# Four rows of a decode page to a partition, position sums over quads, and other buffers for the last value groups

## The chip, the cores and the metric

The kernel runs on one core of one Trainium2 chip. The metric is the device time of one execution in microseconds (us). Before the change it is 3598.28 us, the median of three runs (3588.35 to 3599.67).

## What is computed

One inference step of a two-layer decoder trunk. In each layer a prompt of 1024 tokens and a sample of 8 sequences with 8 new tokens each go through an input projection, three mixers side by side (retention, stick-breaking attention, forgetting attention), an output projection and a gated per-layer embedding. For the sample, both attentions also read a paged past: 32 pages of 128 rows for each of the 8 sequences, 5 heads of 64 numbers to a row, all in float32. The two formulas that matter here are:

```
z    = q @ k.T / 8                               # k: all 4096 past rows, then the new ones
stick-breaking: A[t,s] = exp(log_sigmoid(z[t,s]) + sum over s < j < t of log_sigmoid(-z[t,j]))
forgetting:     A[t,s] = softmax_s(z[t,s] + C[t] - C[s]),  C = cumulative sum of the log forget values
o    = A @ v
k    = cache_k[layer, page_table[sequence]]      # 32 pages of (128, 5, 64), the same for v
```

Stick-breaking so needs, for each past row, the sum of softplus(z) over all later rows, and forgetting attention the sum of the log forget values over all later rows.

## The kernel before

The program is written by engine: SP and POOL mostly issue DMAs, PE (TensorE) does matmuls and transposes, ACT and DVE move results out of PSUM and do elementwise work. Semaphores order them. A layer has eight phases; two of them are the decode stages, one for each kind of attention ("sb" for stick-breaking, "fox" for forgetting). With two layers there are four decode stages in a run.

**Loads.** A page is 128 rows of 320 numbers. Keys are loaded by SP (`load_k`, line 553), a few of the first sequence by ACT (line 1536), values by POOL (`load_group`, line 730). Eight pages make a group, four groups a sequence. Page p of a group lands in columns p*320 to p*320+319 of a buffer, one row to a partition on all 128 partitions. There are two key buffers (`ringK`, one in the weights' tile W, one in the tile named branch) and two value buffers (`ringV`). A key group's load waits until the blocks of the group two before it have been turned (`kt_ready`, line 551), a value group's until the group two before it has been weighed (`v_used`, line 728). The last sequence's value groups 2 and 3 are loaded by SP into the key buffers, which are free by then (lines 572 to 577).

**Keys to scores.** PE turns each group in five blocks of 128 key numbers by four pages (`turn_blocks`, line 1117), taken from PSUM by ACT (line 1548) or DVE (line 2069). It multiplies them with the queries (`score`, line 1139); ACT copies the result out (line 1556), PE turns it again so that the rows of a page lie on partitions (`turn_rows`, line 1153), and DVE puts it into `zs`, 128 partitions by 40 query rows by 33 slots, a slot being a page and the last one the new rows (`drain`, lines 2081 to 2088).

**Scores to weights.** For stick-breaking, DVE and ACT make softplus(z) (`soft`), and DVE's scan over the slots from the last to the first makes `later`, the sum over this and all later slots on the same partition (line 2107). `fold` (lines 1169 and 1170) adds for each row what lies on other partitions: six matmuls of 440 columns, three with the triangular constant `earlier` on `soft` and three with minus one on `later`. DVE adds the result to `zs` (line 2119) and ACT takes the exponential (line 1571). For forgetting attention, `page_sums` and `forget_sums` make the sums within and over the pages once a stage, PE turns them in ten transposes (`turn_forget`, line 1100) and DVE copies them out (line 2012); per sequence there is one small matmul in `fold` (line 1176). `weigh` (line 1202) multiplies the weights with a value group: 40 small matmuls to a group on four strips of PE.

**Order of the work.** All engines run `sequence(b, b - 1, b - 2)` in a loop. PE turns and scores the keys of sequence b, and in between folds and weighs groups 0 to 2 of sequence b-1 and group 3 of sequence b-2. PE's order in a pass is written out by hand (lines 1223 to 1258). The first sequence has nothing before it. After the loop PE weighs group 3 of sequence 6, folds sequence 7 and weighs its four groups (lines 1264 to 1268).

Of the kernel before, what the change touches and what calls it, by code (L numbers as in the profile page):

```python
# [24 lines left out]
ALU = mybir.AluOpType  # L25
# [22 lines left out]
GROUPS = PAGES // PG8  # L48
HI = HA * NEW
# [84 lines left out]
def tables():  # L134
# [17 lines left out]
    t["later_page"] = (j // PAGES == i // PAGES) & (j > i)  # L152
# [47 lines left out]
DECODE_STEPS = {"sb": 3, "fox": 5}  # L200
# [33 lines left out]
def step_program(nc, x_prompt, x_sample, state_ret, cache_sb_k, cache_sb_v, cache_fox_k,  # L234
# [10 lines left out]
    with ExitStack() as ctx:  # L245
# [210 lines left out]
        forget_turned = sem("forget_turned")  # L456
        forget_ready = sem("forget_ready")
# [64 lines left out]
        def _(sp):  # L522
# [3 lines left out]
            sp.dma_start(page_rows[:], page_table.rearrange("(a b) p -> (b p) a", a=2),  # L526
                         allow_slow_non_contiguous=True).then_inc(rows_in, 16)
# [18 lines left out]
            def load_k(L, kind, b, g, pages_of_group=PG8):  # L546
# [5 lines left out]
                for p, pg in enumerate(page_numbers(mybir.EngineType.SP, b * PAGES + g * PG8, pages_of_group)):  # L552
                    sp.dma_start(ringK[g % 2][:, p * DA:(p + 1) * DA],  # L553
                                 cache[L, bass.ds(pg, 1)].rearrange("a s h d -> s (a h d)"))\
                        .then_inc(s[f"k{g % 2}"], 16)

            def decode_loads(L, kind):
# [13 lines left out]

                for g in range(2, GROUPS):
                    sp.wait_ge(s["kt_ready"], (SEQS - 1) * BLOCKS + 5 * (g + 1))
                    for p, pg in enumerate(page_numbers(mybir.EngineType.SP, (SEQS - 1) * PAGES + g * PG8, PG8)):
                        sp.dma_start(ringK[g % 2][:, p * DA:(p + 1) * DA],
                                     CACHE[kind][1][L, bass.ds(pg, 1)].rearrange("a s h d -> s (a h d)"))\
                            .then_inc(s[f"v_last{g % 2}"], 16)
# [70 lines left out]
        def _(pool):  # L648
# [17 lines left out]
            pool.wait_ge(rows_in, 16)  # L666
            pool.sem_inc(rows_next, 1)
            with pool.Fori(0, DEPTH) as L:
# [54 lines left out]
                def load_values(kind):  # L723

                    cache = CACHE[kind][1]
                    def load_group(b, g):

                        await_dma(dec[kind]["v_used"], b * GROUPS + g + 1)
                        for p, pg in enumerate(page_numbers(mybir.EngineType.Pool, b * PAGES + g * PG8, PG8)):
                            pool.dma_start(ringV[:, g % 2, p * DA:(p + 1) * DA],  # L730
                                           cache[L, bass.ds(pg, 1)].rearrange("a s h d -> s (a h d)"))\
# [6 lines left out]
                    for g in range(2):  # L738
                        load_group(SEQS - 1, g)
# [56 lines left out]
        def _(pe):  # L796
# [271 lines left out]
            def decode(phase, L):  # L1068
# [24 lines left out]
                def turn_forget():  # L1093

                    for h in range(HA):
                        pe.wait_ge(forget_part, 2)
                        if h >= 2:
                            pe.wait_ge(forget_ready, h - 1)
                        for half in range(2):
                            ins = pe.transpose(ps[:, 6 + h % 2, half * P:(half + 1) * P], page_sum[:, half, h, :],  # L1100
                                               ident)
                        ins.then_inc(forget_turned, 1)

# [17 lines left out]
                def score(b, g):  # L1121
# [11 lines left out]
                    if g == 1 and not is_first(b):  # L1133

                        pe.wait_ge(s["soft_ready"], b)
# [7 lines left out]
                def turn_rows(b, j):  # L1143
# [5 lines left out]
                    elif not is_first(b):  # L1149
# [1092 lines left out]
```

## Time and profile before

| | |
|---|---|
| time, median of 3 runs | 3598.28 us (3588.35 to 3599.67) |
| profiled execution | 3598.73 us, span 3597.2 us |
| PE matmul busy | 3175.1 us, 88% of the span |
| DVE, ACT, POOL busy | 36%, 26%, 20% |
| DMA | 439.67 MB, mean 122 GB/s |
| chain that ended last | PE 30%, issue 6%, DMA 4%, DVE 2%, SP's queue 2% of the span |
| granted TensorE clock, mean | 0.942 |

The profile is of one execution. Busy time is what an engine worked, the span is from the first to the last instruction. "DMA share" in a window is the mean busy share of the 16 DMA engines, so the rate divided by the share is the rate at which they would move data if all were busy. An instruction's line is that of the source; a number after x counts instructions; the brackets at a row's end give the idle time of the engine just before it and what ended it. PEclk is the TensorE clock that was granted, as a share of full speed.

### The profile page before, as it was taken

Reading aid. Unit: us, or ns where it says so; the run is one execution under the profiler, and the core shown is the slowest. Engines: PE = TensorE matmul, PEld = TensorE weight load, DVE = VectorE, ACT = ScalarE, POOL = GpSimd, SP = SyncE. Lnnn points to the kernel's source line nnn. Section 1 sums busy time; section 2 is a strip of 40 time slices with the busy share of each in tenths; the row PEclk is TensorE's granted clock in tenths of the full one; section 3 lists DMA queues with packets and bytes.
Section 4 is the critical chain, followed back from the end, with each engine's and each line's share of the span. In section 5 each row is a group of like instructions: output and inputs, shape, how many; then the busy total and the mean of one; then the engine's idle time right before and its main releaser. Section 6 shows DMA issues by size and latency. Waiting matters only on the chain. (4 is left out here: it accounts for less than half of the span.)

```text
span 3597.2 us, 67796 instructions
## 1 busy us (share of the span) xinstructions
PE 3175.1 (88%) x25256; PEld 1967.1 (55%) x25256; DVE 1310.9 (36%) x2842; ACT 939.9 (26%) x1740; POOL 709.8 (20%) x1250
## 2 busy tenths in 40 slices
PE   6999989888889788799989999988889887877998
PEld 4566655455656455444455566655556554554443
DVE  3225055444324444211241350644443244442221
ACT  2012233333225333111021121434332253331110
POOL 0000033244210144300000000433441102452000
PEclk9999999999999899899999999999999898998999
DMA  5011102788320598610131011028882206994102
GB/s 170 27 35 35 43 18 73 228 286 280 102 75 1 167 296 281 225 57 14 47 98 33 24 43 49 1 95 260 269 289 63 69 1 220 294 308 155 56 30 73
DMA packets 268656, 439.67 MB, mean 122 GB/s; under 512 B 48817, under 2 KB 216402, under 8 KB 268338
## 3 DMA queue, kind: packets, MB, share of 16 engines
q1 hardware_dynamic: 205810, 239.96, 20.9%
q0 software_dynamic: 55744, 189.25, 16.0%
q10 hardware_dynamic: 6912, 7.87, 0.6%
q8 instruction: 126, 2.06, 0.2%
q14 instruction: 64, 0.52, 0.0%
HBM read 410.28 MB, written 26.65 MB: 121 GB/s over the span
## 5 line engine op out<-in xcount | busy, mean ns | idle before, releaser
L854 PE MATMUL ps<-W,xT 128*128 128x320 f32 (+7 forms) x5120 | 1485.9, 464 | 12.2 <-DVEq L470 11.5
L854 PEld LDWEIGHTS ps<-W,xT 128*128 128x128 f32 (+1 forms) x5120 | 853.5, 183 | 579.1 <-issue 288.5
L730 POOL DMA_DIRECT2D branch<-in_cache_fox_v_dram x480 | 258.9, 539 | 588.3 <-issue 546.7
L730 POOL DMA_DIRECT2D branch<-in_cache_sb_v_dram x480 | 258.4, 538 | 375.7 <-issue 334.9
L1117 PE MATMUL ps<-C,W 128*128 128x128 f32 x1280 | 203.1, 304 | 71.3 <-DMA W<-in_cache_fox_k_dram 25.5
L1548 ACT ACTIVATE branch<-ps 128x512 f32<-128x512 f32 x288 | 165.3, 595 | 360.0 <-PE ps L1117 360.0
L995 PE MATMUL ps<-branch 64*128 64x512 f32 (+7 forms) x480 | 207.9, 560 | 51.3 <-POOLq L470 27.6
L1117 PE MATMUL ps<-C,branch 128*128 128x128 f32 x1280 | 193.4, 294 | 66.7 <-DMA branch<-in_cache_fox_k_dram 23.2
L1202 PE MATMUL ps<-branch 128*8 128x64 f32 x9920 | 183.5, 234 | 63.8 <-DMA branch<-in_cache_fox_v_dram 28.6
L1117 PEld LDWEIGHTS ps<-C,W 128*128 128x128 f32 x1280 | 154.2, 153 | 137.1 <-issue 57.7
L1117 PEld LDWEIGHTS ps<-C,branch 128*128 128x128 f32 x1280 | 146.6, 148 | 148.6 <-issue 100.3
L1139 PE MATMUL ps<-branch,work 128*32 128x512 f32 x896 | 226.7, 625 | 0.8
L1202 PEld LDWEIGHTS ps<-branch 128*8 128x8 f32 x9920 | 159.6, 99 | 88.2 <-issue 34.2
L2069 DVE COPY branch<-ps 128x512 f32<-128x512 f32 x160 | 107.8, 688 | 188.9 <-PE ps L1117 188.9
L1556 ACT ACTIVATE work<-ps 128x512 f32<-128x512 f32 x160 | 92.2, 597 | 316.8 <-PE ps L1139 316.8
L683 POOL DMA_DIRECT2D out_dram<-work x32 | 17.7, 552 | 743.1 <-ACT work L1364 549.0
L995 PEld LDWEIGHTS ps<-branch 64*128 64x128 f32 (+1 forms) x480 | 82.6, 203 | 132.2 <-issue 65.5
L1939 DVE TENSOR_TENSOR_SCAN branch<-branch 128x1024 f32<-128x1024 f32 (+7 forms) x80 | 108.9, 1361 | 77.6 <-POOL branch L720 60.9
L1139 PE MATMUL ps<-W,work 128*32 128x512 f32 x384 | 135.3, 648 | 1.6 <-issue 1.6
L1153 PE MATMUL ps<-C,work 128*128 128x128 f32 x640 | 102.3, 293 | 24.2 <-ACT work L1556 24.2
L2084 DVE COPY branch<-ps 128x64 f32<-128x64 f32 x256 | 46.3, 226 | 203.9 <-PE ps L1153 153.0
L1772 DVE TENSOR_TENSOR work<-ps,branch 128x512 f32<-128x512 f32 (+1 forms) x40 | 25.5, 638 | 250.8 <-PE ps L854 250.5
(244 smaller groups left out, 3380.3 us busy)
## 6 DMA issues: line engine op xcount, KB each, us to landing
branch<-in_cache_sb_v_dram POOLq DMA_DIRECT2D x480, 160.0 KB, 4.4
branch<-in_cache_fox_v_dram POOLq DMA_DIRECT2D x480, 160.0 KB, 4.2
W<-in_cache_sb_k_dram SPq DMA_DIRECT2D x248, 160.0 KB, 3.5
W<-in_cache_fox_k_dram SPq DMA_DIRECT2D x248, 160.0 KB
branch<-in_cache_sb_k_dram SPq DMA_DIRECT2D x240, 160.0 KB, 4.5
branch<-in_cache_fox_k_dram SPq DMA_DIRECT2D x240, 160.0 KB, 4.3
W<-in_w_in_dram SPq DMA_DIRECT2D x14, 1280.0 KB, 6.4
W<-in_w_in_dram SPq DMA_DIRECT2D x9, 1536.0 KB, 7.3
```

The costliest lines, as they stand in the source:

```text
L730: pool.dma_start(ringV[:, g % 2, p * DA:(p + 1) * DA], cache[L, bass.ds(pg, 1)].rearrange("a s h d -> s (a h d)"))\
L854: ins = pe.matmul(out, src[:, k, t * P:t * P + R], W[W_OF[seg]][:, k, a:z], start=(k == 0), stop=(k == kc - 1), **place)
L995: ins = pe.matmul(ps[:, 2 * (u % 2) + c // 512, 0:w], qT[q, a, t * P:(t + 1) * P], kT[q, a, c:c + w], start=True, stop=True)
L1117: ins = pe.transpose(ps[:, n % 2, m * P:(m + 1) * P], ringK[g % 2][:, at:at + P], ident)
L1139: ins = pe.matmul(ps[q:q + 32, bank, :], q_now[:, kk, :], kT_d[(5 * g + kk) % SLOTS], start=True, stop=True, tile_position=(0, q), skip_gr ...
L1153: ins = pe.transpose(ps[:, 6 + j % 2, m * P:(m + 1) * P], z_rows[:, 2 if j == 4 else j % 2, m * P:(m + 1) * P], ident)
L1202: ins = pe.matmul(out(h, a), pr[:, h, :, g * PG8 + first + p], values[:, c:c + HD], start=False, stop=False, tile_position=(0, 32 * a), sk ...
L1548: act.activation(kT_d[n % SLOTS], ps[:, n % 2, :], ACT.Copy).then_inc(s["kt_act"], 1)
L1556: act.activation(z_rows[:, 2 if j == 4 else j % 2, :], ps[:, 3 if j == 4 else (5 if j % 2 else 2), :], ACT.Copy)\
L1939: link(dve.tensor_tensor_scan(prod[:, e:SEQ][:, ::-1], r[:, ::-1], r[:, ::-1], 1.0, ALU.mult, ALU.bypass))
L2069: dve.tensor_copy(kT_d[n % SLOTS], ps[:, n % 2, :]).then_inc(s["kt_dve"], 1)
L2084: dve.tensor_copy(by_pair[:, j, 2 * NEW * kk:2 * NEW * (kk + 1), :, 0], src[:, kk, 0:2 * NEW])
```

## The change

A page now goes to 32 partitions, four consecutive rows to a partition. Page p of a group takes the partitions 32*(p mod 4) onwards and the columns of quad p//4. Four pages, a quad, so lie as 512 consecutive rows, four to a partition, on all 128 partitions. A slot of `zs` is now one of the four rows of a quad, and a quad's four slots on one partition are consecutive rows of the past. The sum over later rows is then `later` on the same partition, which DVE subtracts from `zs` by itself, plus two sums from other partitions that are the same for all four slots of a quad. `fold` makes these in two matmuls of 360 and 320 columns, and DVE subtracts them.

The forget values are laid out alike by DVE's own 32x32 transposes, 40 instructions each waited for. The table of page numbers for the forget values is loaded by four DMAs, one for each place in a quad. Waits of PE for DVE go or get looser, since `fold` now uses one PSUM bank and not three.

Of the last value groups, group 3 of sequence 6 and group 0 of sequence 7 go to the key buffers by SP as soon as the last keys in them are turned, and group 3 of sequence 7 to the first of them by SP once sequence 6 is weighed. Groups 1 and 2 of sequence 7 stay with POOL.

The core of the diff:

```diff
-    t["later_page"] = (j // PAGES == i // PAGES) & (j > i)
+    page_of = QUAD * (r % QUADS) + r // 32
+    t["later_page"] = (j // QUADS % 4 == i // QUADS % 4) & (page_of[:, None] > page_of[None, :])
...
+LAST_VALUES = {(SEQS - 2, 3): (0, 0), (SEQS - 1, 0): (1, 0), (SEQS - 1, 3): (0, 1)}
...
+        def page_place(ring, p):
+            return ring[32 * (p % QUAD):32 * (p % QUAD + 1), p // QUAD * QUAD * DA:(p // QUAD + 1) * QUAD * DA]
+        def page_of(cache, L, pg):
+            return cache[L, bass.ds(pg, 1)].rearrange("a (s r) h d -> s (a r h d)", r=QUAD)
...
-            sp.dma_start(page_rows[:], page_table.rearrange("(a b) p -> (b p) a", a=2),
-                         allow_slow_non_contiguous=True).then_inc(rows_in, 16)
+            by_quad = page_table.rearrange("(x b) (q a) -> a b q x", x=2, a=QUAD)
+            for a in range(QUAD):
+                sp.dma_start(page_rows[32 * a:32 * (a + 1), :], by_quad[a],
+                             allow_slow_non_contiguous=True).then_inc(rows_in, 16)
...
-                    sp.dma_start(ringK[g % 2][:, p * DA:(p + 1) * DA],
-                                 cache[L, bass.ds(pg, 1)].rearrange("a s h d -> s (a h d)"))\
+                    sp.dma_start(page_place(ringK[g % 2], p), page_of(cache, L, pg))\
                         .then_inc(s[f"k{g % 2}"], 16)
...
-                for g in range(2, GROUPS):
-                    sp.wait_ge(s["kt_ready"], (SEQS - 1) * BLOCKS + 5 * (g + 1))
+                for b, g in LAST_VALUES:
+                    place, use = LAST_VALUES[b, g]
+                    if use == 0:
+                        sp.wait_ge(s["kt_ready"], (SEQS - 1) * BLOCKS + 15 + 5 * place)
+                    else:
+                        sp.wait_ge(s["v_used"], 2 + (SEQS - 1) * GROUPS)
...
-                    with pool.Fori(0, SEQS - 1) as b:
+                    with pool.Fori(0, SEQS - 2) as b:
                         for g in range(GROUPS):
                             load_group(b, g)
-                    for g in range(2):
-                        load_group(SEQS - 1, g)
+                    for g in range(3):
+                        load_group(SEQS - 2, g)
+                    for g in (1, 2):
+                        load_group(SEQS - 1, g, (SEQS - 2) * GROUPS + g + 3)
...
-                        for c in range(3):
-                            cols = slice(c * 440, c * 440 + 440)
-                            pe.matmul(ps[:, 5 + c, 0:440], const("earlier"), soft[:, cols], start=True, stop=False)
-                            ins = pe.matmul(ps[:, 5 + c, 0:440], const("negones"), later[:, cols], start=False,
-                                            stop=True)
-                        ins.then_inc(s["expo_ready"], 1)
+                        quads = later.rearrange("p (r s) -> p r s", s=SLOT)[:, :, 0:SLOT:QUAD]
+                        out = ps[:, 6, 0:HI * (QUADS + 1)].rearrange("p (r q) -> p r q", r=HI)
+                        pe.matmul(out, const("before"), quads, start=True, stop=False, skip_group_check=True)
+                        pe.matmul(out[:, :, 0:QUADS], const("earlier"), quads[:, :, 1:], start=False, stop=True,
+                                  skip_group_check=True).then_inc(s["expo_ready"], 1)
...
-                for h in range(HA):
-                    dve.wait_ge(forget_turned, h + 1)
-                    dve.tensor_copy(forget[:, h, :], ps[:, 6 + h % 2, 0:2 * P]).then_inc(forget_ready, 1)
+                dve.wait_ge(forget_part, 2)
+                for half in range(2):
+                    for h in range(HA):
+                        rows_of = page_sum[:, half, h, :].rearrange("p (s r) -> p r s", r=QUAD)
+                        to = forget[:, h, half * P:(half + 1) * P].rearrange("p (j r) -> p r j", r=QUAD)
+                        for k in range(QUAD):
+                            link(dve.transpose(to[:, k, :], rows_of[:, k, :]))
...
+                        dve.wait_ge(s["sum_ready"], b + 1)
+                        link(dve.tensor_tensor(zs, zs, later, ALU.subtract))
...
-                        z3 = zs.rearrange("p (c n) -> p c n", c=3)
-                        dve.tensor_tensor(z3, z3, ps[:, 5:8, 0:440], ALU.add).then_inc(s["soft_ready"], 1)
+                        others = ps[:, 6, 0:HI * (QUADS + 1)].rearrange("p (r q) -> p r q", r=HI)
+                        zq = zr[:, :, 0:PAGES].rearrange("p r (q k) -> p r q k", k=QUAD)
+                        link(dve.tensor_tensor(zq, zq, bc(others[:, :, 0:QUADS], [P, HI, QUADS, QUAD]), ALU.subtract))
+                        dve.tensor_tensor(zr[:, :, PAGES], zr[:, :, PAGES], others[:, :, QUADS], ALU.subtract)\
+                            .then_inc(s["soft_ready"], 1)
```

## Rows read from the trace of the kernel before

**Rows 1.** The page, part 2: DMA busy share in tenths, 40 slices of the span.

```profile
DMA  5011102788320598610131011028882206994102
```

**Rows 2.** Windows over six passes (fox, sb): length, engines' busy, PEclk, DMA share, GB/s.

```profile
3021.98:3231.68 209.70, 171.10 (x2936) 108.23 (x2935) 91.29 (x252) 68.10 (x115) 100.81 (x187) 0.96 0.90 294
2443.50:2668.10 224.60, 195.39 (x2905) 122.46 (x2905) 96.12 (x235) 83.44 (x128) 103.31 (x192) 0.96 0.86 280
```

**Rows 3.** Once-a-pass instructions, seven passes each: count, ns min/median/max, first and last start.

```profile
L2119 DVE TENSOR_TENSOR branch<-branch,ps x7: 1529/1530/1530, 662.6 to 886.4; 128x1320 f32<-128x1320 f32 x7
L2119 DVE TENSOR_TENSOR branch<-branch,ps x7: 1529/1530/1530, 2448.4 to 2668.6; 128x1320 f32<-128x1320 f32 x7
L1176 PE MATMUL ps<-small,C x14: 279/290/300, 1236.7 to 1454.6; 40*128 40x40 f32 x14
L1176 PE MATMUL ps<-small,C x14: 279/290/300, 3022.0 to 3231.8; 40*128 40x40 f32 x14
```

**Rows 4.** Chain of waits in one stick-breaking pass: start us, us, what.

```profile
2538.83 7.55 DMA branch<-in_cache_sb_k_dram
```

**Rows 5.** Timelines of PE and DVE at one fold: start us, us, instruction, idle before.

```profile
2517.35 0.90 PE L1169 MATMUL ps<-branch,C 128*128 128x440 f32 x2
...
2521.04 0.90 PE L1170 MATMUL ps<-branch,C 128*128 128x440 f32 x2
...
2521.98 1.53 DVE L2119 TENSOR_TENSOR branch<-branch,ps 128x1320 f32<-128x1320 f32 x1 [6.60 <-PE ps L1170]
```

**Rows 6.** Timeline of DVE in the first forgetting sequence, five waited-for copies.

```profile
2986.39 1.07 DVE L2039 COPY work<-C 64x64 f32<-64x64 f32 x5
```

**Rows 7.** Timelines of PE and DVE at the end of an sb and a fox stage.

```profile
2693.61 2.32 PE L1202 MATMUL ps<-branch 128*8 128x64 f32 x80 [6.06 <-DMA branch<-in_cache_sb_v_dram]
...
2704.68 2.32 PE L1202 MATMUL ps<-branch 128*8 128x64 f32 x80 [3.04 <-ACT branch L1571]
2708.75 2.33 PE L1202 MATMUL ps<-branch 128*8 128x64 f32 x80 [1.75 <-DMA branch<-in_cache_sb_v_dram]
...
2692.76 2.91 DVE L2107 TENSOR_TENSOR_SCAN branch<-reset,branch 128x1320 f32<-128x1320 bf16 x1
...
3261.93 2.33 PE L1202 MATMUL ps<-branch 128*8 128x64 f32 x80 [2.84 <-DMA branch<-in_cache_fox_v_dram]
...
3270.59 2.33 PE L1202 MATMUL ps<-branch 128*8 128x64 f32 x80 [5.03 <-DMA branch<-in_cache_fox_v_dram]
```

**Rows 8.** DMA queues from 2465 to 2612 us: packets, MB, share (q1 keys, q0 values).

```profile
q1 hardware_dynamic: 18196, 20.71, 43.3%
q0 software_dynamic: 5969, 20.40, 42.8%
```

**Rows 9.** Windows: weights in 2 KB rows, residual in 4 KB rows, one fox pass.

```profile
1714.00:1719.50 5.50, 5.50 (x14) 2.47 (x13) 4.03 (x6) 0.00 (x0) 0.00 (x0) 1.00 0.97 352
...
1811.00:1821.00 10.00, 6.80 (x22) 5.06 (x23) 5.11 (x8) 6.01 (x14) 0.00 (x0) 0.53 0.99 387
...
3136.00:3173.00 37.00, 28.16 (x513) 17.94 (x501) 16.30 (x48) 11.33 (x19) 17.66 (x33) 1.00 0.94 304
```

**Rows 10.** Windows over single residual loads: four on 64 partitions, then two on 128.

```profile
1567.61:1568.39 0.78, 0.78 (x3) 0.35 (x2) 0.00 (x0) 0.00 (x0) 0.00 (x0) 1.00 0.50 168
1634.62:1635.41 0.79, 0.79 (x3) 0.37 (x2) 0.70 (x1) 0.23 (x1) 0.00 (x0) 1.00 0.64 163
3346.00:3346.85 0.85, 0.85 (x4) 0.37 (x3) 0.00 (x0) 0.00 (x0) 0.00 (x0) 1.00 0.59 154
3413.00:3413.81 0.81, 0.81 (x3) 0.37 (x2) 0.71 (x1) 0.23 (x1) 0.00 (x0) 1.00 0.57 159
...
1596.48:1597.84 1.36, 1.36 (x5) 0.60 (x4) 0.00 (x0) 0.49 (x3) 0.00 (x0) 1.00 0.64 203
3314.74:3315.98 1.24, 1.24 (x5) 0.52 (x4) 0.00 (x0) 0.23 (x1) 0.00 (x0) 1.00 0.62 211
```

More of the change, by code:

```diff
@@ L48 @@
 GROUPS = PAGES // PG8
+QUAD = 4
+QUADS = PAGES // QUAD
 HI = HA * NEW
@@ L570, in decode_loads @@
                         load_k(L, kind, b, g)
-                for g in range(2, GROUPS):
-                    sp.wait_ge(s["kt_ready"], (SEQS - 1) * BLOCKS + 5 * (g + 1))
[L574 to L577, printed above, removed]
+                for b, g in LAST_VALUES:
[4 more added lines that the diff above has]
+                        sp.wait_ge(s["v_used"], 2 + (SEQS - 1) * GROUPS)
+                    for p, pg in enumerate(page_numbers(mybir.EngineType.SP, b * PAGES + g * PG8, PG8)):
+                        sp.dma_start(page_place(ringK[place], p), page_of(CACHE[kind][1], L, pg))\
+                            .then_inc(s[f"v_last{place}"], 16)
             def load_decoded(L, kind):
@@ L665, in _ @@
                 pool.wait_ge(arrived_x, 16)
-            pool.wait_ge(rows_in, 16)
+            pool.wait_ge(rows_in, 16 * QUAD)
             pool.sem_inc(rows_next, 1)
@@ L1091, in new_scores @@
                                       start=True, stop=True).then_inc(page_carry, 1)
-                def turn_forget():
-                    for h in range(HA):
[L1096 to L1102, printed above, removed]
                 def turn_blocks(b, blocks):
@@ L1148, in turn_rows @@
                         pe.wait_ge(s["z_drained"], 5 * b + j - 1)
-                    elif not is_first(b):
+                    elif j == 0 and not is_first(b):
                         pe.wait_ge(s["soft_ready"], b)
@@ L1190, in weigh @@
                         pe.wait_ge(s["o_emptied"], b + 1)
-                    if isinstance(b, int) and b == SEQS - 1 and g >= 2:
-                        values = ringK[g % 2]
-                        pe.wait_ge(s[f"v_last{g % 2}"], PG8 * 16)
+                    if isinstance(b, int) and (b, g) in LAST_VALUES:
+                        place, use = LAST_VALUES[b, g]
+                        values = ringK[place]
+                        pe.wait_ge(s[f"v_last{place}"], PG8 * 16 * (use + 1))
                     else:
                         values = ringV[:, g % 2]
-                        pe.wait_ge(v_in[kind][g % 2], PG8 * 16 * (b * 2 + g // 2 + 1 + L * (SEQS * 2 - 1)))
+                        per_layer = SEQS * 2 - 1 - g % 2
+                        ahead = b * 2 + g // 2 + 1
+                        if isinstance(b, int) and b == SEQS - 1:
+                            ahead = per_layer
+                        pe.wait_ge(v_in[kind][g % 2], PG8 * 16 * (ahead + L * per_layer))
                     for first in range(0, PG8, 4):
@@ L1236, in sequence @@
                         fold(before)
-                    elif kind == "fox":
-                        turn_forget()
                     turn_blocks(b, range(10, 13))
                     if before is None and kind == "fox":
-                        pe.wait_ge(forget_ready, HA)
+                        pe.wait_ge(forget_part, 2)
                     turn_rows(b, 0)
```

17 lines of the change are left out of this document (5 added, 12 removed).

## The prediction

> **What bounds the kernel now.** I read the page's second part first: DMA is busy at 8 to 9 tenths in four stretches and nearly idle elsewhere [rows 1]. These are the four decode stages (stick-breaking and forgetting attention, in each of two layers), and all but a few instructions of the diff lie in them. Next the windows over six whole passes of the sequence loop, one of each kind [rows 2]: PE is busy 171.1 of 209.7 us and 195.4 of 224.6 us, the DMA engines 0.90 and 0.86 of the time. Both are near full and neither is. The loop's period comes from the first and last start of an instruction that runs once a pass, seven starts, six periods [rows 3]: (886.4-662.6)/6 = 37.3 and 36.7 us for stick-breaking, 36.3 and 35.0 us for forgetting, mean 36.3. Stick-breaking has about 4 us more PE work a pass and is only 1.4 us longer, so PE alone does not set the period. The chain of waits says what does: the last page of a key group is issued and lands 7.55 us later, and until then PE has no blocks to turn [rows 4]. Of those 7.55 us the transfer of 160 KB itself is a small part; the page stands in line behind the others. A pass moves 64 pages of 128 x 320 x 4 bytes, 10.49 MB. Rate over busy share is 294/0.90 and 280/0.86, both 326 GB/s with the engines full [rows 2], so a pass is 10.49/0.326 = 32.2 us of DMA work against a period of 36.3. The reader is to see a loop with little slack in DMA: a lower rate would become the period at once.
>
> **The change, part by part.** Sums are made against the profiled execution, 3598.7 us (span 3597.2), which is 0.4 us over the median of the three runs, 3598.3.
>
> Fold of the position sums (stick-breaking). Six matmuls of 440 columns become two of 360 and 320. The six start at 2517.35, and the last starts 3.69 us later, so one is 0.74 us and all are 4.43, or 1.68 ns a column [rows 5]. The new two are 680 x 1.68 = 1.14 us. Their moving operand is read with a stride of four elements, for which no row exists; a bound is twice that, 2.3 us. I take 1.14, since the rows give PE's time by columns. Saved: 3.3 us a pass, at the least 2.1. For it DVE gets a subtraction over 1320 columns, 1.53 us like the addition of the same shape, and the addition becomes two instructions, about 0.2 us more. The subtraction runs while DVE would stand idle, 6.60 us, for PE's fold [rows 5]; if PE reaches the rows before DVE is done, it costs some 0.3 us. So PE's part of the path gets 3.0 us shorter.
>
> Forget sums (forgetting attention, once a stage). PE's ten transposes and their hand-over with DVE go. DVE makes 40 small transposes, each waited for. Five waited-for copies of 64x64 took 1.07 us, 0.21 each [rows 6], so 40 are 8.6 us. They run while keys of group 2 are still arriving; with that cover gone they cost some 6 us more than now. I take +1 us a stage, +2 in all, bounds 0 and +12. Three more small loads of the page table at the start go out on SP while the constants load: nothing.
>
> Last five value groups. Today sequence 6's last group lands late, PE waits 6.06 us, and only then folds; the next wait is for the exponentials [rows 7]. In the forgetting stage the waits are 2.84 and 5.03 us [rows 7]. Now that group goes to a key buffer as soon as its last keys are turned, and sequence 7's groups 1 and 2 no longer queue behind it. The stick-breaking chain is then held by DVE: its scan ends at 2692.76+2.91 = 2695.7 [rows 7], a short fold 1.4, the addition 1.7, ACT 1.3, so weighing starts at 2700.3 and not 2704.7, and a further wait of 1.7 us in it goes: -6. In the forgetting stage fold and exponentials come 2.7 us earlier and the waits among the last groups go: -8. Twice each: -28 us; SP's one wait more has nothing behind it but the next stage's weights. If transfers are slower, I count -24.
>
> Page layout. The bytes and the number of DMAs stay, so SP's and POOL's issue time stays. Each page goes to 32 partitions with 5120 contiguous bytes on each, where it went to 128 with 1280. Two effects, of opposite sign.
>
> First, larger pieces. In the loop the key queue moved 20.71 MB in 43.3% and the value queue 20.40 MB in 42.8%, though the value queue's packets were three times as large (3418 bytes on average against 1138) [rows 8]. Per byte they cost the same, so I expect nothing from larger key packets; the other bound is the rate of weights in 2 KB rows, 352/0.97 = 363, and of the residual in 4 KB rows, 387/0.99 = 391 GB/s [rows 9]. The Trainium skill (DMA: Bandwidth & Descriptors, Why small descriptors are slow) counts three fixed cycles a packet beside one per 32 bytes; for 1280 against 5120 bytes that would be some 5% of the keys' half, 0.8 us a pass, and the two queues' equal shares do not show it.
>
> Second, fewer partitions. The nearest rows are the residual's loads for the 64 sample rows, which write 64 partitions and not 128: 168/0.50, 163/0.64, 154/0.59 and 159/0.57, that is 336, 255, 261 and 279, mean 283 GB/s with the engines full; two loads of the same rows on 128 partitions gave 317 and 340 [rows 10]. So half the partitions cost some 14%. A page uses a quarter, but pages go round the four quadrants and two queues run beside each other, so on average more than one quadrant is being written. I take 283. Bounds: 391 above, 255 below, and for strictly half the paths see the rivals.
>
> The sum. 10.49/0.283 = 37.1 us of DMA work a pass. The engines' highest share in a whole pass was 0.94 [rows 9]; 37.1/0.94 = 39.4 us, +3.1 on 36.3. The passes with both queues busy are seven a stage, 28: +87 us. The shorter fold is hidden under it. The first sequence loads keys alone; two of its groups are waited for, some 0.6 us later each: +5. Forget sums +2, last groups -24. Together +70: **3669 us**. By the lowest single row, 255, the pass is 43.7 us and the time 3790; at 300 GB/s it is 3612.
>
> **The rivals.**
>
> No loss from the layout. The rate stays at 326 or above. A stick-breaking pass goes to 37.0 - 3.0 = 34.0 us, for which 32.2 us of work is a share of 0.95, so 34.2: -39 over 14 passes. With the last groups and the forget sums that is -65. If larger pieces lift the keys to some 377 GB/s, work is 30.0 us, the period 33.6, and the forgetting stages gain 0.5 a pass: -81, **3518 us**. For it: the 64-partition loads are short bursts, and one of the four ran at 336. Against it: the other three.
>
> Half the paths. If the engines pair up on the partitions of a page, and both queues keep step in that, sixteen engines do what eight do now. Eight at the best rate seen are 391/2 = 195 GB/s: 53.8 us of work, a pass of 57 us, +585: about **4170 us**. Its place is the same queue of pages before PE's turns. Against it: no 64-partition load was that low. The Trainium skill (SBUF — State Buffer, Door 1: The DMA port swizzle) says so: partitions 0 to 63 reach only eight of sixteen ports and 64 to 127 the other eight, some 27 GB/s each. By its figure eight ports carry 218 GB/s, a pass would be 51 us and the time 4000. My rows agree in direction and not in size.
>
> Balance. The point from which the loss decides is the rate at which 28 passes lose what the last groups give, 0.6 us each: 36.9 x 0.94 = 34.7 us, 302 GB/s. Between 299 and 306 the change is lost in what a measurement of this kernel can tell, 0.3% or 11 us.
>
> **Chances.** The forecast's case 0.42, its own range 3612 to 3790. No loss 0.40: three rows of four speak against it, but they are bursts of 64 pieces and the loop has two queues. Half the paths 0.10. Balance 0.08. Faster by over 0.3%: 0.40; within: 0.08; slower: 0.52. The range must hold 8 in 10, with cases of both signs: from 3490, some 25 us under the best case, to 3860, between the forecast's upper bound and the half-paths case, which is left out.
>
> **What would show each step.** In the changed profile: the loop's DMA share at 0.93 or more with the rate under 290 GB/s says the layout costs; a share under 0.86 says it pays. The period from starts one pass apart: 39.4, against 34 for no loss. The page issue on the chain of waits longer than 7.55 us, or gone. Fold matmuls of 360 and 320 columns starting 0.5 to 0.7 us apart; 1 us or more says the stride costs. DVE's idle time before the addition near zero. At the stages' ends no wait of 5 or 6 us for values. The forecast is wrong if the engines hold 326 GB/s or more on 32 partitions; then PE's shorter fold comes through.

## The result and the profile after

The change makes the kernel slower: **3877.0 us**, median of 4 runs (3874.4 to 3885.4), against 3596.3 us for the kernel before beside it on the chip (4 runs). The ratio is 1.079 [1.076, 1.081]. The profiled execution has a span of 3873.8 us. From the page of the kernel after, parts 1 to 4:

```profile
PE 3250.8 (84%) x25108; PEld 2019.2 (52%) x25108; DVE 1356.6 (35%) x2944; ACT 940.2 (24%) x1740; POOL 646.4 (17%) x1218
...
DMA  4001105999320899920120101079991128998101
GB/s 166 30 24 41 42 1 141 235 226 224 79 65 6 205 230 226 212 71 15 44 91 30 42 24 42 1 190 229 227 222 44 58 53 191 225 223 206 56 31 68
...
q1 hardware_dynamic: 107554, 245.21, 25.5%
q0 software_dynamic: 54208, 184.01, 20.0%
...
PE 27%; DMA 9%; issue 5%; SPq 2%; DVE 1%; ACT 1%; POOL 1%; POOLq 0%; ACTq 0%; DVEq 0%
```

The four decode stages stand out as before, now at nine tenths in all their middle slices [rows 1]. The chain that ended last has 9% of DMA where it had 4%. Next, windows of the kernel after over six passes, stick-breaking, then forgetting (columns as in [rows 2]):

```profile
2585.80:2855.60 269.80, 205.45 (x2844) 127.77 (x2844) 107.41 (x247) 82.99 (x126) 93.51 (x192) 0.84 1.01 228
3229.60:3502.00 272.40, 190.32 (x2881) 125.18 (x2884) 91.00 (x249) 67.27 (x112) 90.05 (x184) 0.83 0.99 222
```

The share rose from 0.86 and 0.90 to 1.0, and the rate fell from 280 and 294 to 228 and 222 GB/s. The DMA engines are never free, and move less. PE's granted clock is 0.83 to 0.84 where it was 0.96, and its busy time is larger though it has less to do. A once-a-pass instruction of each kind of stage, and the wait for a key group in the chain, of the kernel after:

```profile
L2130 DVE TENSOR_TENSOR branch<-branch,ps x7: 1486/1487/1489, 2585.8 to 2855.6; 128x1280 f32<-128x1280 f32 x7
L1178 PE MATMUL ps<-small,C x14: 279/290/300, 3229.2 to 3506.0; 40*128 40x40 f32 x14
```

```profile
2602.78 13.21 DMA branch<-in_cache_sb_k_dram
```

The periods are 269.8/6 = 45.0 and 276.8/6 = 46.1 us, against 36.7 and 35.0 [rows 3]. The last page of a key group lands 13.21 us after its issue, against 7.55 [rows 4].

**Where the time went.** I cut each stage at three instructions: DVE's clearing of the new keys' buffer (start), DVE's last step before the exponentials of the first and of the eighth sequence, and PE's sum over the decoded rows (end). Summed over the four stages, in us:

| | before | after | difference |
|---|---|---|---|
| start to the first sequence's step | 190.6 | 220.5 | +29.9 |
| seven passes to the eighth's step (28 in all) | 1004.4 | 1233.1 | +228.7 |
| from there to the end | 62.0 | 76.2 | +14.2 |
| four stages | 1257.0 | 1529.8 | +272.8 |

The profiled spans differ by 276.6, so nearly all of it lies in the decode stages. A pass costs 8.2 us more on average over the seven. The first six take 45.0 to 46.1 us in all four stages. The seventh takes only 35 to 39; the last key load is issued at its start (2858.0 us in the second stick-breaking stage).

### The profile page after: what moved, and what is told of

Same layout as the page of the kernel before. It is cut to its first block and busy times, and to the rows that moved or that the text cites. A ratio compares the mean times of both kernels' runs of the same rounds, so it can differ in the third digit from the quotient of the medians.

```text
span 3873.8 us, 67565 instructions
## 1 busy us (share of the span) xinstructions
PE 3250.8 (84%) x25108; PEld 2019.2 (52%) x25108; DVE 1356.6 (35%) x2944; ACT 940.2 (24%) x1740; POOL 646.4 (17%) x1218
## 5 line engine op out<-in xcount | busy, mean ns | idle before, releaser
L1123 PE MATMUL ps<-C,W 128*128 128x128 f32 x1280 | 229.8, 335 | 167.6 <-DMA W<-in_cache_fox_k_dram 87.4
L1123 PE MATMUL ps<-C,branch 128*128 128x128 f32 x1280 | 223.1, 328 | 158.9 <-DMA branch<-in_cache_sb_k_dram 83.0
L746 POOL DMA_DIRECT2D branch<-in_cache_fox_v_dram x464 | 227.3, 490 | 753.1 <-issue 703.8
L746 POOL DMA_DIRECT2D branch<-in_cache_sb_v_dram x464 | 227.3, 490 | 509.0 <-issue 456.2
L1123 PEld LDWEIGHTS ps<-C,W 128*128 128x128 f32 x1280 | 176.2, 170 | 244.8 <-issue 153.2
L1123 PEld LDWEIGHTS ps<-C,branch 128*128 128x128 f32 x1280 | 169.3, 165 | 247.2 <-issue 191.9
L1209 PE MATMUL ps<-branch 128*8 128x64 f32 x9600 | 196.1, 248 | 73.0 <-DMA branch<-in_cache_fox_v_dram 33.5
L1142 PE MATMUL ps<-branch,work 128*32 128x512 f32 x896 | 248.4, 685 | 2.2 <-issue 1.5
L1209 PEld LDWEIGHTS ps<-branch 128*8 128x8 f32 x9600 | 171.1, 105 | 100.2 <-DMA branch<-in_cache_fox_v_dram 37.5
L1142 PE MATMUL ps<-W,work 128*32 128x512 f32 x384 | 155.5, 743 | 1.6 <-issue 1.6
L1156 PE MATMUL ps<-C,work 128*128 128x128 f32 x640 | 108.1, 304 | 24.4 <-ACT work L1560 24.2
L2092 DVE COPY branch<-ps 128x64 f32<-128x64 f32 x256 | 46.1, 225 | 213.7 <-PE ps L1156 157.1
```

The source lines that it names most:

```text
L746: pool.dma_start(page_place(ringV[:, g % 2], p), page_of(cache, L, pg))\
L1123: ins = pe.transpose(ps[:, n % 2, m * P:(m + 1) * P], ringK[g % 2][:, at:at + P], ident)
L1142: ins = pe.matmul(ps[q:q + 32, bank, :], q_now[:, kk, :], kT_d[(5 * g + kk) % SLOTS], start=True, stop=True, tile_position=(0, q), skip_gr ...
L1156: ins = pe.transpose(ps[:, 6 + j % 2, m * P:(m + 1) * P], z_rows[:, 2 if j == 4 else j % 2, m * P:(m + 1) * P], ident)
L1209: ins = pe.matmul(out(h, a), pr[:, h, :, g * PG8 + first + p], values[:, c:c + HD], start=False, stop=False, tile_position=(0, 32 * a), sk ...
```

## The experiments

### The two halves of the change apart

e1_one_row is the kernel after with the old placement in its two helpers. e2_layout_alone is the kernel before with the new placement in all its page loads, and nothing else of the change. In both, the position sums go over other rows than they should, with the same instructions. The edit of the first:

```diff
-            return ring[32 * (p % QUAD):32 * (p % QUAD + 1), p // QUAD * QUAD * DA:(p // QUAD + 1) * QUAD * DA]
+            return ring[:, p * DA:(p + 1) * DA]
-            return cache[L, bass.ds(pg, 1)].rearrange("a (s r) h d -> s (a r h d)", r=QUAD)
+            return cache[L, bass.ds(pg, 1)].rearrange("a s h d -> s (a h d)")
```

> The changed kernel, but every page is loaded as before the change, one row of 1280 bytes to each of 128 partitions; the new fold, the new buffers for the last values and DVE's forget transposes stay. The rows then stand in another order than the position sums assume, so the sums are over other rows; the number and shape of all instructions is as in the changed kernel. Theory P (the loss is the transfer rate of pages that go to 32 neighbouring partitions): the loop's rate over share goes back from 230 to about 326 GB/s, the period of a stick-breaking pass to about 34 us, the time to 3520 (3500 to 3560). Rival W (the loss is in the new waits and orders: DVE's subtraction and transposes, the values' new buffers): the time stays above 3750.

> The kernel before, with one edit: each page is loaded as in the changed kernel, four rows to a partition on 32 partitions. The computation is otherwise that of before, so it adds up rows in another order. Theory P: the DMA share in the loop 0.98 or more at 225 to 232 GB/s, a period of 45 us as in the changed kernel, since the fold is hidden under the transfers, and about 20 us more than the changed kernel for the last value groups: 3880 to 3930. Rival W: below 3700.

With the old placement and all the rest of the change: 3568.5 us, ratio 0.992 [0.990, 0.995], 8 us above the range that I had given. With the new placement alone: 3899.6 us in one run. So the placement is the whole loss, +303 us by itself. The rest of the change is a small gain: 28 us beside the old placement, not the 65 to 81 of the rival without loss, and 22.6 us beside the new one (3899.6 to 3877.0). Windows of one row to a partition, forgetting, then stick-breaking:

```profile
2987.40:3199.20 211.80, 173.47 (x2828) 112.42 (x2828) 90.79 (x251) 68.63 (x114) 95.40 (x178) 0.93 0.86 283
2418.00:2625.00 207.00, 175.03 (x2748) 106.56 (x2747) 105.96 (x243) 80.89 (x127) 94.76 (x177) 0.98 0.88 288
```

Rate over share is 329 and 327 GB/s, as before [rows 2].

### Which partitions, or how many

Two placements differ from the kernel after in `page_place` alone, or in `page_place` and the number of rows in `page_of`. The first, e3_every_fourth, keeps 32 partitions and 5120 bytes on each, but takes every fourth partition. The second, e6_two_rows, gives a page 64 neighbouring partitions with two rows on each, the lower half for even pages and the upper for odd ones.

```diff
-            return ring[32 * (p % QUAD):32 * (p % QUAD + 1), p // QUAD * QUAD * DA:(p // QUAD + 1) * QUAD * DA]
+            return ring[p % QUAD:P:QUAD, p // QUAD * QUAD * DA:(p // QUAD + 1) * QUAD * DA]
...
+            return ring[64 * (p % 2):64 * (p % 2 + 1), p // 2 * 2 * DA:(p // 2 + 1) * 2 * DA]
...
+            return cache[L, bass.ds(pg, 1)].rearrange("a (s r) h d -> s (a r h d)", r=2)
```

> The changed kernel, but a page's 32 partitions are every fourth one (page a of a quad takes partitions a, a+4, a+8 and so on) and not 32 neighbours. Pieces stay 5120 bytes, and the number of partitions stays 32. The position sums keep the constants for the old order, so they are over other rows. Theory P (what costs is that the 32 neighbours are served by half of the paths into the memory): a page now uses all of them, two engines still meet now and then; 270 to 326 GB/s, 3520 to 3680. Rival L (what costs is the length of a piece on one partition, or the small number of partitions): as the changed kernel, 230 GB/s and about 3877.

> The changed kernel, but a page goes to 64 neighbouring partitions, two rows (2560 bytes) to each, alternately the lower and the upper 64. The position sums are over other rows than meant. Theory P: the lower 64 partitions have the same half of the paths as the lowest 32, so nothing is gained: 225 to 240 GB/s, 3840 to 3900. Rival L (number of partitions or length of a piece): half way between 230 and 326, some 280 GB/s and 3650 to 3700, as the prediction took it.

Every fourth partition: 3594.8 us, ratio 1.000 [0.998, 1.001]. The loss is gone, but for 26 us against one row to a partition (3568.5), with the same number of partitions and the same pieces. So neither is its cause: it is that the 32 partitions are neighbours. Two rows: 3792.1 us in one run. That lies between what theory P said there (3840 to 3900, nothing gained) and what rival L said (3650 to 3700), and it took the runs with another order of pages, below, to place it. Windows of every fourth partition, its queues from 2432 to 2642 us, then the window of two rows:

```profile
2432.00:2642.00 210.00, 177.88 (x2657) 108.52 (x2658) 102.91 (x232) 80.05 (x124) 90.53 (x172) 0.93 0.79 278
3009.20:3224.30 215.10, 173.43 (x2824) 112.72 (x2824) 90.15 (x251) 68.06 (x114) 90.53 (x178) 0.93 0.81 278
```

```profile
q1 hardware_dynamic: 8999, 30.72, 41.5%
q0 software_dynamic: 8067, 27.55, 37.5%
```

```profile
2570.00:2760.00 190.00, 143.19 (x2109) 92.14 (x2110) 80.12 (x173) 61.27 (x92) 71.32 (x139) 0.87 1.03 245
```

Every fourth partition moves 278/0.79 = 352 and 278/0.81 = 343 GB/s with the engines full, more than one row to a partition. The reader can get the mean time that an engine spent on 5120 bytes from a queue's row: 16 engines x 210 us x 0.415 over 30.72 MB is 0.232 us for the keys. The same sum for the kernel before [rows 8] gives 0.252 us for the same bytes in pieces of 1280, 8% more. How much of that is the size of the pieces is not shown: the values had packets of the same size in both kernels (3418 and 3415 bytes on average), and theirs fell alike, from 0.253 to 0.234 us, beside the keys on the same engines. The commonest time of a piece in these two traces, 0.055 us for 1280 bytes, so 0.220 for four, and 0.196 for 5120, says that larger ones do cost less. In the kernel after, from 2590 to 2800 us, the keys' 23.71 MB took 50.0% of 210 us, 0.363 us for 5120 bytes:

```profile
q0 software_dynamic: 6887, 23.56, 50.1%
q1 hardware_dynamic: 6955, 23.71, 50.0%
```

Every fourth partition is 26 us slower than one row to a partition, though it has less DMA work. A part of the answer may lie with SP. Its rows for the issue of one page, every fourth partition, two rows, one row, and the kernel after:

```profile
L567 SPq DMA_DIRECT2D W<-in_cache_sb_k_dram x248: 472/472/1264, 452.2 to 2653.7; - x124
```

```profile
L567 SPq DMA_DIRECT2D W<-in_cache_sb_k_dram x248: 468/469/1374, 452.4 to 2796.9; - x124
```

```profile
L567 SPq DMA_DIRECT2D W<-in_cache_sb_k_dram x248: 332/337/1551, 451.9 to 2632.0; - x124
```

```profile
L567 SPq DMA_DIRECT2D W<-in_cache_sb_k_dram x248: 319/320/1354, 452.7 to 2845.4; - x124
```

Eight pages so take 1.1 us more of SP (8 x 0.135), and the issue of key pages is 16.9% of the chain of waits from 3080 to 3160 us, where one row to a partition has 11.3% from 3060 to 3140. That this eats the gain is an argument from the chain; no run took it away.

### The order of the pages

If the loss is in the halves of the partitions, it must change with the order in which pages are issued, while each still lies where the change puts it. After the change, two pages that follow each other (0 and 1, 2 and 3) lie in the same half.

e7_alternate goes through the pages of a group in another order, in all four places where pages are loaded; e10_opposite does the same but for the values in POOL's queue, whose order is 2, 0, 3, 1, 6, 4, 7, 5. The first edit:

```diff
+        def in_turn(numbers, first=0):
+            pages_in = dict(enumerate(numbers, first))
+            return [(p, pages_in[p]) for p in (0, 2, 1, 3, 4, 6, 5, 7) if p in pages_in]
...
-                for p, pg in enumerate(page_numbers(mybir.EngineType.SP, b * PAGES + g * PG8, pages_of_group)):
+                for p, pg in in_turn(page_numbers(mybir.EngineType.SP, b * PAGES + g * PG8, pages_of_group)):
```

> The kernel after, with the pages of every group issued in the order 0, 2, 1, 3, 4, 6, 5, 7 for keys and values, so that two pages that follow each other lie in opposite halves of the partitions; each page still lies where it lies after the change, and all is computed as there. Theory P (a page on neighbouring partitions reaches half the paths, and two pages in the same half one behind the other leave the other half idle): as with two rows to a partition on 64 partitions, 245 GB/s at a share of 1.0, 3780 to 3810 us. Rival Q (32 partitions are a narrower mouth than 64, and the order does not matter): 226 to 230 GB/s, 3865 to 3890. Rival R (two opposite pages are always in flight and the loss vanishes): 3565 to 3600.

> As the kernel after with alternating order (pages 0, 2, 1, 3, ... for the keys), but the values in the order 2, 0, 3, 1, 6, 4, 7, 5, so that the two queues would write opposite halves if they kept in step; all is computed as after the change. Theory P says the two queues then use all paths as far as they keep in step: somewhere from 3600 us (always in step) to 3797 (no better than with the same order in both queues). Since the groups of the two queues start at moments that nothing ties together, I expect no better than the same order: 3780 to 3810 us at 245 GB/s. A rival, that one page in flight to a quarter of the partitions fills all that there is, would also give 3797.

Alternating: 3797.0 us, ratio 1.055 [1.052, 1.059], 80 us less than after the change from the order alone. Opposite order in the two queues: 3789.8 us in one run. Their windows:

```profile
2560.00:2750.00 190.00, 144.49 (x2120) 90.67 (x2121) 82.31 (x183) 61.83 (x95) 70.72 (x144) 0.87 1.00 245
```

```profile
2560.00:2750.00 190.00, 143.42 (x2025) 90.75 (x2018) 80.39 (x185) 61.52 (x93) 70.48 (x144) 0.86 1.01 242
```

The order matters, so Q (a narrow mouth, whatever the order) falls, and theory P stands in that the halves matter; its 245 GB/s was taken over from the run with two rows and not derived. The 245 GB/s is that of two rows on 64 partitions: once consecutive pages lie in opposite halves, it is all the same whether a page has a quarter or a half of the partitions. But R falls too: the share stays at 1.0, and most of the loss remains. The second row shows that the two queues can't be set against each other by their order.

### One narrow queue

e8_keys_narrow is the kernel after with the values of POOL's queue one row to a partition:

```diff
-                            pool.dma_start(page_place(ringV[:, g % 2], p), page_of(cache, L, pg))\
+                            pool.dma_start(ringV[:, g % 2, p * DA:(p + 1) * DA],
+                                           cache[L, bass.ds(pg, 1)].rearrange("a s h d -> s (a h d)"))\
```

> The kernel after, with the values of POOL's queue one row to a partition and the keys as they are after the change (the weights then meet other value rows than the reference's). Half the bytes go to 32 partitions. If times of the two kinds just add (10.49 MB as 5.24/0.226 + 5.24/0.326 = 39.3 us, at a share of 0.97 a pass of 40.5): 3568 + 28 x 4.2 = 3685 us (3665 to 3700). If the wide value pages fill the paths that the narrow key pages leave idle: 3570 to 3630 and a share under 0.97. If a narrow page holds every engine up, as much as after: above 3750.

3769.8 us in one run. Window and queues of it, then the values' queue of one row to a partition from 2418 to 2625 us:

```profile
2560.00:2750.00 190.00, 145.35 (x2052) 91.11 (x2051) 82.19 (x174) 63.61 (x97) 77.50 (x144) 0.89 0.99 247
```

```profile
q1 hardware_dynamic: 6704, 22.90, 51.1%
q0 software_dynamic: 7021, 23.98, 47.8%
```

```profile
q0 software_dynamic: 8252, 28.20, 41.3%
```

Three theories stood here, and none fits whole. The time lies where the third one put it, above 3750. The passes are near the first one, in which the times of narrow and wide pages add: the seven passes of the four stages take 1137.8 us, 40.6 a pass, against its 40.5. The total beside it, 3685, was made from a wrong base: I took 36.3 us a pass for a kernel with the new sums, where one row to a partition has 965.3/28 = 34.5; with that, 3568 + 28 x 6.1 = 3739. The first sequences and the stages' ends add 15, and another 15 lie outside the decode stages in this one execution.

But the DMA engines' own time is not the sum of the two kinds. If it were, they would move 10.49/39.3 = 267 GB/s when full; 247/0.99 is 249, about half way down to the 226 of two narrow queues. By the sum above, 5120 bytes of a value page took 0.310 us here and 0.248 with all pages wide, and those of a key page 0.347 where two narrow queues took 0.363. So the wide values did not use what the narrow keys left idle, they were slowed by them. The share of 0.99 says that the engines were held, not unused.

### The two gains by themselves

e4_values_alone is the kernel before with `LAST_VALUES`, its loads on SP, POOL's loops and PE's waits as after the change. e5_sums_alone is e1_one_row with these as before. The lines that they exchange on SP, taken from the first:

```diff
-                for g in range(2, GROUPS):
-                    sp.wait_ge(s["kt_ready"], (SEQS - 1) * BLOCKS + 5 * (g + 1))
...
+                for b, g in LAST_VALUES:
+                    place, use = LAST_VALUES[b, g]
+                    if use == 0:
+                        sp.wait_ge(s["kt_ready"], (SEQS - 1) * BLOCKS + 15 + 5 * place)
+                    else:
+                        sp.wait_ge(s["v_used"], 2 + (SEQS - 1) * GROUPS)
```

> The kernel before with one part of the change alone, the five last value groups in other buffers; everything is computed as before. The forecast's term was -6 us in a stick-breaking stage and -8 in a forgetting stage, -28 in all: about 3568 to 3572 us against 3596. The rival: with the rows one to a partition, the stick-breaking stages gained 17 us each and the forgetting stages nothing, from this part and the shorter sums together. If the value groups carry all of that, this run has both stick-breaking stages at some 300 us and the forgetting ones unchanged, about 3565. If the sums carry it, the value groups are worth under 3 us a stage here, 3585 to 3595.

> The kernel after with pages one row to a partition (so the sums over later rows and the weights belong to other rows than the reference's) and with the value groups' buffers of before: the shorter fold and the forget sums are what is left of the change. By the forecast's terms: nothing or -39 us for the fold, according to whether DMA or PE holds the pass, and +2 for the forget sums. Theory now: fold -10 us in a stick-breaking stage, forget sums +5 to +10 in a forgetting stage because nothing covers DVE's 40 transposes, about 3590 us (3582 to 3600). Rival: forget sums cost nothing and the fold gains -3 us a pass where PE leads, then 3560 to 3570.

The value groups: 3593.5 us, ratio 0.9989 [0.9971, 1.0007], so between a gain of 10 us and a loss of 3, as the last of the three cases said. The sums: 3582.8 us, ratio 0.996 [0.995, 0.998], a gain of 13. Stage by stage, in us (one profile each; the kernel before has 319.7, 312.1, 316.4, 308.8):

| | sb | fox | sb | fox |
|---|---|---|---|---|
| value groups alone | -2.5 | -8.6 | -3.2 | -0.2 |
| sums alone | -13.0 | +5.5 | -14.7 | +3.3 |
| both, one row to a partition | -18.6 | -2.2 | -15.0 | +2.9 |

PE's timeline at the end of the second stick-breaking stage, value groups alone:

```profile
2675.51 1.31 PE L1214 MATMUL ps<-W,branch 128*8 128x64 f32 x80
2676.75 0.39 PE L1221 MATMUL ps<-v_new,branch 64*8 64x64 f32 x10
2684.10 1.84 PE L1176 MATMUL ps<-branch,C 128*128 128x440 f32 x2 [6.96 <-DVE branch L2119]
...
2690.50 0.90 PE L1177 MATMUL ps<-branch,C 128*128 128x440 f32 x2
2694.36 2.35 PE L1214 MATMUL ps<-branch 128*8 128x64 f32 x153 [2.96 <-ACT branch L1583]
```

two windows of it:

```profile
2684.00:2691.00 7.00, 6.90 (x12) 3.29 (x12) 0.40 (x3) 0.00 (x0) 3.07 (x6) 0.62 0.63 193
2691.00:2704.00 13.00, 6.04 (x333) 4.95 (x332) 1.99 (x3) 1.30 (x1) 0.00 (x0) 0.96 0.01 4
```

and the same fold in the kernel before, first and last row:

```profile
2696.39 1.57 PE L1169 MATMUL ps<-branch,C 128*128 128x440 f32 x2
...
2700.74 0.90 PE L1170 MATMUL ps<-branch,C 128*128 128x440 f32 x2
```

The wait of 6.06 us for sequence 6's last values [rows 7] is gone, and in its place stands one of 6.96 us for DVE's scan. The wait for values had hidden most of that one: in the kernel before the scan ended at 2695.67 and the fold began at 2696.39, so it could begin only 0.7 us sooner. The six matmuls of the fold then run from 2684.10 to 2691.40, 7.3 us at a mean granted clock of 0.62, so for the most part at 1.2 and not 2.4 GHz, after PE had stood still for 6.96 us. In the kernel before they ran from 2696.39 to 2701.64, 5.3 us, right behind 2.3 us of weighing [rows 7]. Two microseconds went there.

The end of a stage can be measured from where DVE lets PE go: the end of sequence 7's scan (stick-breaking) or of its row maximum (forgetting), up to PE's sum over the decoded rows, in us:

| | sb | fox | sb | fox |
|---|---|---|---|---|
| before | 19.1 | 24.8 | 19.4 | 25.1 |
| value groups alone | 20.4 | 19.9 | 19.8 | 19.5 |
| sums alone | 18.1 | 25.4 | 18.5 | 24.8 |
| both, one row to a partition | 15.0 | 19.6 | 15.0 | 20.9 |
| placement alone | 24.6 | 26.4 | 22.6 | 28.0 |
| the kernel after | 19.1 | 24.4 | 19.6 | 24.4 |

In the forgetting stages the value groups do their work alone, some 5 us each. In the stick-breaking stages the sums alone gain 1 us, and both parts together 4.3 us each.

DVE's transposes in the forgetting stage, sums alone, and PE's wait behind them:

```profile
2969.82 11.70 DVE L2011 STREAM_TRANSPOSE work<-branch 128x32 f32<-128x32 f32 x40
```

```profile
2982.30 1.97 PE L1119 MATMUL ps<-C,W 128*128 128x128 f32 x8 [4.32 <-DVE branch L2068]
```

The 40 take 11.70 us, 0.29 each, in one stretch. Keys had arrived by 2971.76, in the midst of it, and from 2977.98 on PE stood for 4.32 us, since DVE has to take the turned blocks out of PSUM. The fold, in two passes of sums alone:

```profile
2504.42 1.32 PE L1168 MATMUL ps<-branch,C 128*128 128x360 f32 x2
2505.56 1.31 PE L1169 MATMUL ps<-branch,C 128*128 128x320 f32 x2
2540.32 1.32 PE L1168 MATMUL ps<-branch,C 128*128 128x360 f32 x2
2541.47 1.31 PE L1169 MATMUL ps<-branch,C 128*128 128x320 f32 x2
```

The second starts 1.14 us after the first: 3.2 ns a column at full clock (the granted clock was 1.00 from 2503 to 2506 us), against 1.68 [rows 5]. The first of them writes its result densely as those of before did, so what differs a column is the moving operand, read four elements apart: it costs nearly twice as much. It is the sign that the prediction had named, 1 us or more between the two starts. The whole fold is 2.45 us, against 4.6.

## Why the prediction was wrong in size

**What bounds the kernel** was right: a loop with little slack in DMA, in which a lower rate becomes the period at once. The share went to 1.0 and the period followed the rate.

**The layout's direction** was right, and so was the place: the page on the chain of waits. That pages one row to a partition move 326 GB/s held as well.

**The failed step** is the size of the term "Second, fewer partitions". I took 283 GB/s, the mean of four short loads onto 64 partitions, and a pass of 39.4 us. The loop ran at 222 to 228. Two readings were behind it. I held that pages going round the four quadrants, with two queues, would spread over more than one quadrant "on average". But two pages in a row lie in the same half, and even when they don't, the rate is only 245; a narrow page in one queue also slows the other's wide pages (0.310 against 0.248 us). And I read a rate over a share in windows of 0.8 us in which the share was 0.50 to 0.64 [rows 10]; a short burst with half-idle engines did not bound what a loop with full ones does. I had also kept a share of 0.94 as the highest; the loop holds 1.0 when nothing but DMA bounds it. With 226 GB/s and the share of 1.0 in the same sum, a pass is 46.4 us, +283 for 28 passes, and the time 3865. That this lands 12 us from the measured time is in part luck: the 28 passes cost 229 more and not 283, since the first six of a stage grew by 9.0 us each and not by 10.1, and the seventh by 3.2, while the first sequences and the stages' ends cost 44 where the sum has -17. (The prediction's own sum at 300 GB/s gives 3607 and not 3612.)

**The rival that was nearest in mechanism** is half the paths. Its 4170 us from my rows is further off than the forecast's 3669. Its rate was too low, 195, half of that of the residual's loads in 4 KB rows [rows 9]. Half of 418 (16 engines, 5120 bytes each in 0.196 us, the commonest time of such a piece in the trace with every fourth partition) is 209 GB/s, and what was measured is a little above.

The Trainium skill (SBUF — State Buffer, Door 1: The DMA port swizzle) gives eight ports some 218 GB/s, and the runs agree in kind and nearly in size: 226 with neighbours in one half, no loss of rate (343 to 352) with 32 partitions spread over both. Its figure was the best estimate of the rate that I had, and I gave its case 1 in 10.

**The first sequence** was put at +5, and the forget sums at +2; together they cost 29.9 us in the four stages. With one row to a partition 9.6 of them are there too (14.3 more in the forgetting stages, 4.8 less in the others), so some 20 come with the placement, at whose low rate the first keys arrive.

**The last groups** were put at -24. The 14.2 us that the ends are longer than before hide what they gave, since the slow transfers lengthen the ends too. The fair comparison is with the new placement alone: the rest of the change took off 22.6 us, beside the -22 that I had put for last groups and forget sums together (what the shorter fold gave is in it too). And the ends, from the scan or the row maximum, are 14 us shorter in all. PE still waits for values at the end of the stages of the kernel after:

```profile
2904.91 2.59 PE L1209 MATMUL ps<-branch 128*8 128x64 f32 x78 [3.28 <-DMA branch<-in_cache_sb_v_dram]
```

```profile
3556.99 2.33 PE L1209 MATMUL ps<-branch 128*8 128x64 f32 x80 [6.63 <-DMA branch<-in_cache_fox_v_dram]
```

So a sign that I had named, no wait of 5 or 6 us for values, did not come. With fast transfers, both parts of the change shorten the ends by 18 us (4.2, 5.3, 4.4 and 4.2), against the forecast's 28. The buffers alone gave 5 us and not 28 in time. They lack the short fold of 1.4 us, with which the term's stick-breaking half was worked out from the scan's end; what the term did not name is that the fold then runs at a low clock behind an idle PE (0.62 with the buffers alone, 0.50 from 2665.8 to 2669.0 us with both parts and one row to a partition).

**The fold** was put at 3.3 us saved a pass, at the least 2.1. It is the lower end: 14.0 us less over seven passes with the sums alone, 2.0 a pass. I had taken the price a column from a dense operand. In the kernel after it was nearly hidden under DMA, as said: a stick-breaking period of 45.0 us against 45.9 with the placement alone. **The forget sums** were put at +1 a stage. With the sums alone the time up to the first sequence's step grew by 7.1 and 4.4 us in the two forgetting stages, inside the bound of 12 in all; one transpose took 0.29 us where the copies that I went by took 0.21, and the cover, the keys of group 2, was shorter than the work.

The two gains and the transfers do not add up to a version that is clearly faster and still computes what the reference does: the value groups alone are that, and no faster than can be told. The shorter fold needs four consecutive rows on a partition; every fourth partition would give that with other constants and another way to lay out the forget values, and its time, with the sums over other rows, was that of the kernel before. Such a kernel was not built. It also stays open how the two halves share the engines, and so why alternating pages get to 245 GB/s and not further.

## What to carry to other kernels

Before a transfer is laid out anew, ask which partitions one DMA touches, and not only how many bytes lie in one piece: with the same 32 partitions and the same pieces of 5120 bytes, neighbours gave 226 GB/s and every fourth partition 350. Take the rate for such a question from a burst long enough to fill the engines, and where none exists, let the range reach to the halved rate. Where a wait at the end of a stage is taken away, ask what it had hidden, and at what clock PE goes on after standing still. And compare a part of a change beside the rest as it is in the kernel after too: the last groups look like a loss against the kernel before, and are a gain against the placement alone.

## What the runs showed of the hardware beyond that

- Issuing one page took SP 320 ns with 32 neighbouring partitions, 337 with 128, and 469 and 472 with 64 neighbours of two rows or 32 partitions four apart. Neither the stride nor the number of partitions alone explains it, and it stays open.
- Most often a piece of 1280 bytes took 0.055 us of an engine and one of 5120 bytes 0.196, so 11% less a byte. In the loop the means of the keys were 0.252 and 0.232 us for 5120 bytes; I had expected no difference.
- A queue of pages on neighbouring partitions also slowed a queue of pages on all partitions beside it, by a quarter (0.248 to 0.310 us for 5120 bytes), and both together moved 249 GB/s with the engines full, where adding the two kinds' times gives 267.
- A matmul whose moving operand is read four elements apart took 3.2 ns a column, against 1.68 for a dense one, at the full clock.
